# A fused transformer block on one core: first loads on one queue, joint column sums, and four modulation units moved from TensorE to VectorE

## The chip, the cores and the metric

The kernel runs on one core of a Trainium2 chip. The metric is the device time of one execution in microseconds (us). The core has TensorE (PE: matmuls; PEld is its weight load), VectorE (DVE), ScalarE (ACT), GpSimd (POOL), and the queues through which transfers are issued: SP's own (SPq) and ScalarE's (ACTq). Matmuls write to PSUM, eight banks of 128 x 512 float32; everything else lies in SBUF.

## What is computed

The input is x (256 tokens of 1024) and one conditioning row c of 1024. All arithmetic is float32. Cut to what matters here:

```python
mod = silu(c) @ w_ada + b_ada                    # 1024 x 6144, twelve units of 512 columns
shift1, scale1, gate1, shift2, scale2, gate2 = split(mod, 6)
h = rmsnorm(x) * norm1_w * (1 + scale1) + shift1
r_q, r_k, r_v, r_g, d_q, d_k, d_v, d_z, d_a, d_b = split(h @ w_in)
ret = retention(rotary(r_q), rotary(r_k), r_v)   # 4 heads of 128, chunks of 128
qkv = silu(causal_dwconv([d_q, d_k, d_v], conv_w))
dn  = gated_delta_rule(l2norm(q), l2norm(k), v, g, beta)   # inverse of (I + A) per chunk of 64
x = x + gate1 * (concat(ret, dn) @ w_out)
h2 = rmsnorm(x) * norm2_w * (1 + scale2) + shift2
x = x + gate2 * moe(h2)                          # 32 experts, top 2 of one group, 6 MB each
# then a pooling mixer and a convolutional feed-forward layer on the result
```

Units 0 and 1 of `mod` are shift1, 2 and 3 scale1, 4 and 5 gate1, 6 and 7 shift2, 8 and 9 scale2, 10 and 11 gate2.

## The kernel before

The program of each engine is written out by hand, with counting semaphores between the engines (`mm` counts TensorE's finished groups, `vd` VectorE's, `ad` ScalarE's). Tokens lie in two groups of 128 (index n).

**Slots and loads.** Weights come in units of 2 MB into eight slots: five of `ring` (0 to 4; slot 3 is HIGH, slot 4 is FIFTH) and three of `arena`. `units.place` fixes each unit's slot, and `sync_program` (L2392 and on) issues the loads in one written order on SP's queue; before each it waits until the slot's former unit has been used (`used`). The first three transfers (constants C, `first_cols` with c in it, and x) are issued by ScalarE (L1899 to L1901), and SP waits for `first_cols` between units 0 and 1. Behind the modulation units 0 to 3 come the delta units dn 1, dn 0 and dn 2 (keys, queries, values), the small loads, the retention units proj 2, 0, 1, and then modulation units 4 to 7, each once its slot is free.

**A modulation unit on TensorE** (`ada`, L540 to L553). The column of silu(c) is spread to 32 columns (`crep`), and eight matmuls (16 instructions, since one of float32 takes two) leave four partial rows of 512 in four row groups of a PSUM bank. The partial rows are copied to `part` (`spread_out` on VectorE for units 0 to 3, L1252; `ada` on ScalarE for the others, L1909) and summed over partitions by a matmul: with `sel` as weights for the gates (`gate_total`, L556), and for shift and scale with the data as weights, so that the result is a column (`column_total`, L561: eight matmuls of 64 weight columns for each half, over the view `by_eights`, which the copy has put in another order). `turn_over(n)` issues n matmuls whose results nobody reads.

**The start.** TensorE does units 0 to 3 with the transposes of the normed rows between, VectorE makes modc (shift and scale), and both VectorE and ScalarE write hT, the modulated and transposed input.

**Delta projections** (`delta_project`, L604). Twelve blocks of 16 matmuls, dn 1, dn 0, then the small gates `ab`, then dn 2. Behind each block VectorE runs a convolution of four dependent instructions from PSUM (`delta_conv`, L1281 to L1290) and ScalarE a silu. Then come norms, gates and cumulated decays ("gc", "dec", "bt", "at").

**PSUM banks.** `take` hands the banks out in turn; a take waits until the group that had the bank eight takes before (leaving kept ones out) has been read, which its reader tells by `free`. In the order of takes, "dec" of n = 0 and 1 have banks 5 and 6, "bt" 7 and 0, "at" 1 and 2, and the first retention projection 3 and 4. "dec" is read by the eight subtractions at L1331 on VectorE.

**The inverse, in levels.** For each chunk, levels 1 to 6 follow each other: "pm" (TensorE), its copy PM (ScalarE, L2026), "xm" and "xt" (TensorE), and their subtraction from XM and XTD (VectorE, L1393 and L1399). "pm" of a level needs XM of the level before, and the masked factor of its level, which GpSimd makes (`masked`, L2316 on). The retention projections (`project`, 24 matmuls of 512 columns each) are put between as filler for TensorE, and before the change so were units 4 (end of level 2), 5 (level 3), 6 (level 4) and 7 (in level 5 between "pm" and "xm"). The projections use float32 split in two parts: ScalarE makes the high one (`higher`, L1940) and VectorE the low one (`lower`, L1237).

**GpSimd's order** in this stage: `masked(2)`, `masked(3)`, `rotate(0, 0)`, `rotate(0, 1)`, `masked(4)`, `rotate(1, 0)`, `rotate(1, 1)`, `masked(5)`. A `rotate` is six instructions of 128 x 256 on a projected and copied block of queries (0) or keys (1); `turn_rotated` on TensorE waits for both token groups of it. "pm" of level 5 waits for `masked(5)`.

**Behind it** come scores, the output projection, the router, the experts (each of 32 with 6 MB of weights through the eight slots), and the feed-forward layer.

A take, as TensorE does it:

```python
            def take(*name, keep=False):                       # L483
                b, k = banks.take(name, keep)
                if k > 1:
                    pe.wait_ge(bank_free[b], k - 1)
```

## Time and profile before

| what | us |
|---|---|
| three executions | 916.0, 918.78, 918.87 |
| their median | 918.78 |
| the profiled execution | 919.4 |
| its span, first to last instruction | 917.6 |
| TensorE busy in the span | 893.3 (97%) |
| VectorE / ScalarE / GpSimd busy | 410.6 / 314.3 / 106.2 |
| mean share of the 16 DMA engines, by the queues | 80% |

The span is 1.8 us short of the time of the profiled execution. TensorE is busy nearly all the time, so what counts is where it waits, what it does that could be left out, and at which of its two clock levels it does it.

### The profile page before, as it was taken

The page shows a single profiled execution, that of the slowest core. Times are in us where ns is not written, and L with a number is a line of the kernel's source. Part 1 is how long each engine was busy: PE and PEld are TensorE (multiplying, and loading weights), DVE is VectorE, ACT ScalarE, POOL GpSimd, SP SyncE. Part 2 cuts the span into 40 slices and gives each one's busy share as a digit, 9 for nine tenths or more (in the row PEclk, how much of TensorE's full clock was granted, in tenths as well). Part 3 has the DMA queues.
Part 4 walks back from the last instruction along what each step waited for, and adds up shares of the span by engine and source line. Part 5 has one row for each costly group of instructions (what it writes and reads, how often), then busy time and mean ns, then how long its engine had stood idle before and what let it go on. Part 6 is the DMA issues. An engine that isn't in the chain of part 4 may idle for free.

```text
span 917.6 us, 13421 instructions
## 1 busy us (share of the span) xinstructions
PE 893.3 (97%) x5530; PEld 575.9 (63%) x5530; DVE 410.6 (45%) x697; ACT 314.3 (34%) x507; POOL 106.2 (12%) x116
## 2 busy tenths in 40 slices
PE   5999999999999999999999999999998999999998
PEld 2688876777644434444344444444435899999886
DVE  2357725368522323222223232223234778888643
ACT  1227335342522222322222212222213555555531
POOL 1024463031000000000000000000000022222200
PEclk9999999999999999999999999999999999999999
DMA  9962259787999899999999999999999665555301
GB/s 353 415 291 93 93 193 355 282 326 292 398 402 419 313 420 421 421 419 420 420 421 418 419 421 420 423 419 419 421 421 357 217 194 183 180 179 184 128 1 47
DMA packets 60892, 289.47 MB, mean 315 GB/s; under 512 B 4500, under 2 KB 28692, under 8 KB 33688
## 3 DMA queue, kind: packets, MB, share of 16 engines
q1 hardware_dynamic: 59104, 284.13, 78.3%
q10 hardware_dynamic: 1720, 4.40, 1.2%
q8 instruction: 46, 0.75, 0.3%
q14 instruction: 22, 0.18, 0.1%
HBM read 287.47 MB, written 1.05 MB: 314 GB/s over the span
## 4 chain that ended last, share of the span: by engine, by line
PE 90%; DVE 3%; DMA 3%; issue 2%; ACT 1%; POOL 1%; SPq 0%; ACTq 0%; DVEq 0%
PE ps L1032 24%; PE ps L1056 12%; PE ps L537 8%; PE ps L1020 7%; PE ps L1153 7%; PE ps L1154 7%; PE ps L1155 7%; PE ps L620 4%; PE ps L1072 3%; PE ps L1045 2%; DMA ring<-in_ada_units_dram 2%; PE ps L552 2%; PE ps L520 2%; DMA S<-in_first_cols_dram 1%; PE ps L511 1%
## 5 line engine op out<-in xcount | busy, mean ns | idle before, releaser
L1035 PE MATMUL ps<-ring,proj 128*64 128x512 f32 x320 | 140.9, 593 | 0.0
L1032 PE MATMUL ps<-ring,proj 128*64 128x512 f32 x304 | 133.9, 593 | 0.0
L1853 DVE TENSOR_TENSOR w_l<-ring,w_h 128x2048 fp32r<-128x2048 f32 x33 | 75.5, 2292 | 44.8 <-ACT w_h L2201 44.8
L1153 PE MATMUL ps<-h_h,w_h 128*128 128x256 f32 x336 | 95.1, 283 | 0.0
L1154 PE MATMUL ps<-h_l,w_h 128*128 128x256 f32 x336 | 95.1, 283 | 0.0
L1155 PE MATMUL ps<-h_h,w_l 128*128 128x256 f32 x336 | 95.1, 283 | 0.0
L1032 PEld LDWEIGHTS ps<-ring,proj 128*64 128x64 f32 x304 | 41.1, 137 | 84.6 <-issue 84.6
L1032 PE MATMUL ps<-arena,proj 128*64 128x512 f32 x208 | 91.6, 593 | 0.0
L2201 ACT CAST w_h<-ring 128x2048 fp32r<-128x2048 f32 x33 | 62.8, 1903 | 81.4 <-PE ps L1155 76.9
L1709 DVE SCALAR_TENSOR_TENSOR RQ<-ps,gate_of,proj 128x512 f32<-128x512 f32 x32 | 24.0, 751 | 147.1 <-PE ps L1057 147.1
L2157 ACT CAST MX_r<-RQ 64x512 fp32r<-64x512 f32 x62 | 38.2, 616 | 143.9 <-DVE RQ L1709 143.1
L1035 PE MATMUL ps<-arena,proj 128*64 128x512 f32 x192 | 84.6, 593 | 0.0
L1697 DVE COPY proj<-ps 128x256 f32<-128x256 f32 x32 | 13.6, 425 | 132.6 <-PE ps L1045 132.6
L2149 ACT ACTIVATE proj<-ps 64x512 f32<-64x512 f32 x32 | 18.9, 590 | 153.1 <-PE ps L1035 153.1
L1056 PE MATMUL ps<-ring,proj 128*64 128x512 f32 x144 | 65.6, 598 | 0.6 <-issue 0.6
L1020 PE MATMUL ps<-hT,proj 128*128 128x128 f32 x512 | 63.2, 284 | 2.5 <-DVE hT L1674 2.1
L1057 PE MATMUL ps<-ring,proj 128*64 128x512 f32 x144 | 65.6, 598 | 0.0
L1032 PEld LDWEIGHTS ps<-arena,proj 128*64 128x64 f32 x208 | 28.2, 137 | 58.2 <-issue 58.2
L1153 PEld LDWEIGHTS ps<-h_h,w_h 128*128 128x128 f32 x336 | 64.5, 192 | 0.0
L1154 PEld LDWEIGHTS ps<-h_l,w_h 128*128 128x128 f32 x336 | 64.5, 192 | 0.0
L1155 PEld LDWEIGHTS ps<-h_h,w_l 128*128 128x128 f32 x336 | 64.5, 192 | 0.0
L1020 PEld LDWEIGHTS ps<-hT,proj 128*128 128x128 f32 x512 | 61.8, 201 | 2.8 <-DVE hT L1674 2.3
(372 smaller groups left out, 1601.7 us busy)
## 6 DMA issues: line engine op xcount, KB each, us to landing
ring<-in_w_dram SPq DMA_DIRECT2D x114, 1024.0 KB, 15.0
arena<-in_w_dram SPq DMA_DIRECT2D x72, 1024.0 KB, 15.7
ring<-in_ada_units_dram SPq DMA_DIRECT2D x11, 2048.0 KB, 8.6
ring<-in_ffn_w_in_dram SPq DMA_DIRECT2D x22, 1024.0 KB, 8.1
ring<-in_in_units_dram SPq DMA_DIRECT2D x6, 2048.0 KB, 23.1
ring<-in_ffn_w_out_dram SPq DMA_DIRECT2D x5, 2048.0 KB, 8.0
arena<-in_in_units_dram SPq DMA_DIRECT2D x2, 2048.0 KB, 24.8
ring<-in_out_units_dram SPq DMA_DIRECT2D x2, 2048.0 KB, 9.2
```

What stands on the lines that cost most here:

```text
L537: i = pe.matmul(ps[:, 0:512], rows_k, w[:, k, :], start=(first and k == 0), stop=(final and k == 3))
L1020: t = pe.matmul(ps[:, o:o + 128], XR[:, n, c * 128:(c + 1) * 128], pick[:, n, :, :].rearrange("p e s -> p (e s)"), start=(n == 0), stop=(n ...
L1032: pe.matmul(ps[0:SLOTS, :], XTe[i % 2][:, k, :], u1[:, k, :], start=(k == 0), stop=(k == 7))
L1035: t = pe.matmul(ps[64:64 + SLOTS, :], XTe[i % 2][:, k, :], u3[:, k, :], start=(k == 0), stop=(k == 7))
L1056: pe.matmul(ps[0:SLOTS, :], HTe[i % 2][:, k, :], w[:, 0:512], start=(k == 0), stop=(k == 3))
L1057: t = pe.matmul(ps[64:64 + SLOTS, :], HTe[i % 2][:, k, :], w[:, 512:1024], start=(k == 0), stop=(k == 3))
L1153: pe.matmul(ps, ah, bh, start=first, stop=False)
L1154: pe.matmul(ps, ah, bl, start=False, stop=False)
L1155: return pe.matmul(ps, al, bh, start=False, stop=final)
L1853: ve.tensor_tensor(low, src, dst.bitcast(F32), ALU.subtract).then_inc(split_ready, 1)
L2157: ac.copy(YB[i % 2][own, j, :], YG[own, :]).then_inc(E.high_rows, 1)
L2201: ac.copy(dst, src).then_inc(w_high, 1)
```

## The change

- The first loads all go through SP's queue, in the order `first_cols`, C, unit 0, x, unit 1, 2, 3, with no wait between. ScalarE issues none of them.
- The view `by_eights` becomes a strided one, so that units are copied to `part` as they are.
- `column_totals` sums both halves of a segment with eight matmuls of 128 weight columns, in place of sixteen of 64. The start keeps its two halves, and one `turn_over(2)` there goes.
- Units 4 to 7 are computed on VectorE: eight dependent instructions of 128 x 512 each (a product, then seven products with a sum), from the unit's slot into `part`. Then the sum over partitions has `ones` as weights. Units 4 and 5 go between the convolutions, unit 6 into level 1 behind `lower(3)`, unit 7 into level 2 behind `lower(5)`.
- `gate_total` of 4 and 5 moves on TensorE from level 4 to before `project(0)`, on VectorE from level 3 to before level 0.
- Units 4 and 5 are loaded among dn 1, dn 0 and dn 2. The slots are given out anew: behind the retention units the roles of slots 0, 2 and FIFTH are exchanged in a ring, in the experts and the last layer too.

```diff
-        by_eights = part_[...].rearrange("k (c p) -> k c p", c=8)
+        by_eights = part_[...].rearrange("k (p c) -> k c p", c=8)
...
-        for name, s in (..., (("dn", 1), R + 1), (("dn", 0), R),
-                        (("dn", 2), FIFTH), (("proj", 2), 0), (("proj", 0), 1), (("proj", 1), 2), (("ada", 4), FIFTH), (("ada", 5), 0),
-                        (("ada", 6), 1), (("ada", 7), FIFTH), (("proj", 3), 2), (("ada", 10), 0), (("ada", 8), 1), (("ada", 9), FIFTH),
-                        (("proj", 4), 0), (("ada", 11), 2), (("wo", 0), 1), (("wo", 1), FIFTH)):
+        for name, s in (..., (("dn", 1), R + 1), (("ada", 4), 0),
+                        (("dn", 0), R), (("ada", 5), 1), (("dn", 2), FIFTH), (("proj", 2), 2), (("proj", 0), 0), (("proj", 1), 1),
+                        (("ada", 6), FIFTH), (("ada", 7), 2), (("proj", 3), 0), (("ada", 10), FIFTH), (("ada", 8), 1), (("ada", 9), 2),
+                        (("proj", 4), FIFTH), (("ada", 11), 0), (("wo", 0), 1), (("wo", 1), 2)):
...
             def gate_total(j, src):
                 ps = take("total", j)
-                pe.wait_ge(*drained("ada", j))
-                pe.matmul(ps[:, :], sel, src, ...)
+                pe.wait_ge(ada_rows, by_vector.index(j) + 1)
+                pe.matmul(ps[:, :], ones, src, ...)
...
             def column_totals(seg):
-                column_total(seg, 1, column_total(seg, 0))
+                ps = take("columns", seg)
+                ...
+                for c in range(8):
+                    i = pe.matmul(ps[:, 2 * c:2 * c + 2], by_eights[:, c, :], (ones if seg == 3 else sel)[:, 0:2], start=True, stop=True)
...
             second = column_total(1, 0)
-            turn_over(2)
             ada(3, ada_half)
...
                 four(("at", n), ...)
+            gate_total(4, part[0])
+            gate_total(5, part[1])
             project(0)
...
                 elif level == 5:
-                    ada(7)
...
                 elif level == 4:
-                    gate_total(4, part[0])
-                    gate_total(5, part[1])
                     turn_rotated(0)
...
                     project(4)
-                    ada(4)
-                elif level == 3:
-                    ada(5)
                 elif level == 4:
                     turn_rotated(1)
-                    ada(6)
...
+            def ada(j, chunks=range(8)):        # VectorE
+                w, dst = unit(("ada", j), 512), part[j % 2]
+                for c in chunks:
+                    if c == 0:
+                        ...
+                        ve.wait_ge(*filled(("ada", j)))
+                        ve.tensor_scalar(dst, w[:, 0, :], ccol[:, 0:1], None, ALU.mult).then_inc(*vd.up("ada", j))
+                    else:
+                        ve.wait_ge(*vd.of("ada", j))
+                        ve.scalar_tensor_tensor(dst, w[:, c, :], ccol[:, c:c + 1], dst, ALU.mult, ALU.add)...
...
-                ve.tensor_copy(by_eights[:, :, 64 * (j % 2):64 * (j % 2) + 64]..., full("ada", j)...)
+                ve.tensor_copy(part[j % 2], full("ada", j)[:, :]).then_inc(*free("ada", j))
...
-            delta_conv(1, range(4))
-            delta_conv(0, range(4))
+            delta_conv(1, range(1))
+            for m in range(1, 4):
+                delta_conv(1, (m,))
+                ada(4, range(2 * m - 2, 2 * m))
+            for m in range(4):
+                delta_conv(0, (m,))
+                ada(4, (6, 7)) if m == 0 else ada(5, range(2 * m - 2, 2 * m))
             ve.tensor_copy(ab_turned, ...)
             delta_conv(2, (0,))
+            ada(5, (6, 7))
...
+            gate_total(4)
+            gate_total(5)
             idb = mid(cst("ident_half"), 4)
...
                 if level == 1:
                     lower(3)
+                    ada(6)
                 elif level == 2:
                     lower(5)
-                elif level == 3:
-                    gate_total(4)
-                    gate_total(5)
+                    ada(7)
...
-            ac.dma_start(C[:, :], I["consts"][:, 0:258]).then_inc(const_in, 16)
-            ac.dma_start(first_cols, I["first_cols"]).then_inc(first_in, 16)
-            ac.dma_start(X[:, :, :], ...).then_inc(x_in, 16)
...
+            sp.dma_start(first_cols, I["first_cols"]).then_inc(first_in, 16)
+            sp.dma_start(C[:, :], I["consts"][:, 0:258]).then_inc(const_in, 16)
             load_ada(0)
-            sp.wait_ge(first_in, 16)
+            sp.dma_start(X[:, :, :], ...).then_inc(x_in, 16)
             load_ada(1)
...
             load_in("dn", 1, 2560)
+            load_ada(4)
             load_in("dn", 0, 2048)
+            load_ada(5)
             load_in("dn", 2, 3072)
...
             load_in("proj", 1, 512)
-            load_ada(4)
-            load_ada(5)
             load_ada(6)
```

ScalarE's copies of units 4 to 7 go too, and its copies of 8 and 9 become plain ones.

## Rows read from the trace of the kernel before

**Rows 1.** Windows: busy us of each engine with instructions, granted PE clock, DMA share, GB/s

```profile
34.70:82.00 47.30, 47.21 (x222) 38.61 (x222) 25.27 (x60) 20.49 (x35) 8.19 (x17) 1.00 0.57 235
...
500.00:600.00 100.00, 100.00 (x514) 43.98 (x512) 29.24 (x53) 23.02 (x47) 0.00 (x0) 1.00 1.01 421
```

**Rows 2.** Line L2454, second half of unit 3, issued at 11.3 us: time to landing

```profile
DMA to landing us min/median/max: 18.4/18.4/18.4
```

**Rows 3.** Tile arena, 0 to 40 us: loads dn 1 (first) and dn 0, landing

```profile
L2433 SPq DMA_DIRECT2D arena<-in_in_units_dram x2: 452/454/456, 12.0 to 12.5; - x2
DMA to landing us min/median/max: 22.6/24.8/27.0
```

**Rows 4.** Windows of the start, columns as in rows 1

```profile
11.00:12.00 1.00, 1.00 (x6) 0.20 (x8) 0.00 (x0) 0.00 (x0) 0.00 (x0) 1.00 0.75 160
...
14.00:16.00 2.00, 1.90 (x13) 0.69 (x5) 1.04 (x3) 0.28 (x2) 0.91 (x3) 1.00 0.97 410
```

**Rows 5.** VectorE in order of time: start us, us, line, operation

```profile
63.27 0.48 DVE L1285 TENSOR_SCALAR arena<-ps,S 128x256 f32<-128x256 f32 x1 [1.42 <-PE ps L620]
...
71.72 0.17 DVE L1296 COPY S<-ps 128x16 f32<-128x16 f32 x1 [1.76 <-PE ps L638]
```

**Rows 6.** VectorE by form: count, total us, mean ns

```profile
L1317 DVE SCALAR_TENSOR_TENSOR arena<-arena,MX 128x1024 f32<-128x1024 f32 x2 | 2.4, 1220 | 3.4 <-ACT MX L1975 3.4
```

**Rows 7.** TensorE in order of time: start us, us, line, operation

```profile
87.69 3.36 PE L537 MATMUL ps<-ring_r,vrow_r 128*128 128x512 f32 x12
...
99.28 1.15 PE L520 MATMUL ps<-consts,arena 64*64 64x64 f32 x32
...
103.02 1.15 PE L520 MATMUL ps<-arena 64*64 64x64 f32 x32 [0.23 <-POOL arena L2325]
...
127.53 1.92 PE L552 MATMUL ps<-ring,S 128*32 128x512 f32 x16
129.38 1.15 PE L520 MATMUL ps<-arena 64*64 64x64 f32 x32
...
141.16 1.98 PE L559 MATMUL ps<-part,consts 128*128 128x512 f32 x4
...
148.83 1.15 PE L520 MATMUL ps<-arena 64*64 64x64 f32 x32
...
158.44 1.14 PE L752 MATMUL ps<-arena 64*64 64x64 f32 x16
```

**Rows 8.** TensorE, column sums at 172 us (64 weight columns), list sums at 247 us (128)

```profile
172.07 1.82 PE L566 MATMUL ps<-consts,part 128*64 128x2 f32 x32
...
247.27 0.98 PE L926 MATMUL ps<-part,S 128*128 128x32 f32 x8
```

**Rows 9.** VectorE in order of time, 89 and 122 us

```profile
89.69 2.15 DVE L1331 TENSOR_SCALAR arena<-ps,S 128x128 f32<-128x128 f32 x8
...
122.59 2.69 DVE L1240 TENSOR_TENSOR ring_r<-ring,ring_r 128x2048 fp32r<-128x2048 f32 x1
```

**Rows 10.** GpSimd in order of time, levels 2 to 4

```profile
118.76 2.84 POOL L2337 TENSOR_TENSOR S<-proj,S 128x256 f32<-128x256 f32 x4 [10.54 <-ACT proj L1987]
...
123.21 4.75 POOL L2337 TENSOR_TENSOR S<-proj,S 128x256 f32<-128x256 f32 x4
...
129.41 1.41 POOL L2325 TENSOR_TENSOR arena<-arena,consts 128x256 f32<-128x256 f32 x2
135.21 2.80 POOL L2337 TENSOR_TENSOR S<-proj,S 128x256 f32<-128x256 f32 x4 [4.38 <-ACT proj L1987]
...
143.83 1.42 POOL L2325 TENSOR_TENSOR arena<-arena,consts 128x256 f32<-128x256 f32 x2
```

**Rows 11.** ScalarE in order of time, the copy of "pm" of level 5

```profile
150.05 0.65 ACT L2026 COPY arena<-ps 128x256 f32<-128x256 f32 x2
```

**Rows 12.** Windows around a wait of TensorE in the experts, columns as in rows 1

```profile
488.90:491.00 2.10, 0.07 (x1) 0.00 (x0) 0.48 (x3) 0.18 (x1) 0.00 (x0) 1.00 0.99 414
491.00:497.00 6.00, 5.93 (x35) 5.85 (x36) 1.39 (x4) 1.93 (x6) 0.00 (x0) 0.72 1.01 415
```

More of the change, by code:

```diff
@@ L557, in gate_total @@
                 ps = take("total", j)
-                pe.wait_ge(*drained("ada", j))
-                pe.matmul(ps[:, :], sel, src, start=True, stop=True).then_inc(*mm.up("total", j))
+                pe.wait_ge(ada_rows, by_vector.index(j) + 1)
+                pe.matmul(ps[:, :], ones, src, start=True, stop=True).then_inc(*mm.up("total", j))
             def column_total(seg, half, ps=None):
@@ L571, in column_totals @@
             def column_totals(seg):
-                column_total(seg, 1, column_total(seg, 0))
+                ps = take("columns", seg)
+                for half in range(2):
+                    if seg == 3:
+                        pe.wait_ge(ada_rows, by_vector.index(2 * seg + half) + 1)
+                    else:
+                        pe.wait_ge(*drained("ada", 2 * seg + half))
+                for c in range(8):
+                    i = pe.matmul(ps[:, 2 * c:2 * c + 2], by_eights[:, c, :], (ones if seg == 3 else sel)[:, 0:2], start=True, stop=True)
+                i.then_inc(*mm.up("columns", seg, 0))
+                mm.at["columns", seg, 1] = mm.n
             def eights(src, c):
@@ L794, in tensor_program @@
                     ada(10)
-                else:
+                elif level == 6:
                     project(7)
@@ L1910, in ada @@
                 ps, dst = full("ada", j), part[j % 2]
[L1911 to L1915 removed]
+                if j in (8, 9):
+                    ac.wait_ge(*mm.of("columns", 3, 1))
                 elif j > 9:
                     dst = late_part[j % 2]
[L1918 to L1924 removed]
+                ac.copy(dst, ps[:, :]).then_inc(*free("ada", j))
             ac.wait_ge(*vd.of("scale1"))
```

40 lines of the change are left out of this document (15 added, 25 removed).

## The prediction

> **What bounds the kernel now.** I read the windows first. From 34.7 us on TensorE is busy for 47.21 of 47.30 us, and in the experts for 100 of 100 us, while the DMA share is 0.57 and 1.01 [rows 1]. So work taken from TensorE ahead of the experts shortens the run, unless something else is then late. In the experts both TensorE and the transfers are full. Their loads start when slots come free in TensorE's order, and the slots there are only renamed, so I take the experts and all behind them to shift rigidly with the start of the experts.
>
> Next the start. The second half of unit 3 is issued at 11.3 us and lands 18.4 us later, at 29.7 [rows 2]. The first delta unit, dn 1, is issued at 12.0 and lands at 34.6 [rows 3], just when the first delta projection starts (34.67). The sum of unit 3 and the delta load end together, and each must be earlier for a gain.
>
> Then TensorE in order of time [rows 7] and, beside it, GpSimd [rows 10] and VectorE [rows 5, 9]. TensorE runs from 103 to 158 us with no wait. GpSimd works from 118.76 to 130.82 on the first two rotations and `masked(4)`, is idle to 135.21, and works to 145.25 on the last two rotations and `masked(5)` [rows 10]. "pm" of level 5, which needs `masked(5)`, starts at 148.83 [rows 7]. This slack of 3.6 us is what the change uses up.
>
> Measurements of this kernel tell about 0.3%, 2.8 us, from no change. All times below are on the clock of the profiled execution before.
>
> **The start.** With one queue and no wait, the dip at 11 to 12 us goes: 160 GB/s where 410 are moved soon after [rows 4], 0.25 MB or 0.6 us. The order of the other bytes is nearly as before. Bounds: nothing, if x now stands ahead of what it used to run beside; and 2.8 us, as follows. From 12.0 to 34.6 us some 9.3 MB move at 410 GB/s, but units 1 to 3 and dn 1 are only 8.4 MB; 0.9 MB, 2.2 us, is of later loads that run ahead on some of the engines [rows 3, 4]. If the single queue ended that too, it would be 0.6 + 2.2. I take 0.7 us, near the lower end, because those loads are all on SP's queue before as well. The plain copies and the `turn_over(2)` less lie where TensorE waits for unit 3: nothing.
>
> By the Trainium skill (DMA: Bandwidth & Descriptors, "Issuing engines are not separate DMA queues") transfers of all issuing engines run on the same 16 DMA engines and interleave; by that, putting them on one queue would give no more than the dip.
>
> **VectorE among the convolutions.** A chunk of a unit is a product with a sum over 128x512, both inputs in SBUF. The same operation over 128x1024 takes 1.22 us [rows 6]; halved, with some 0.16 us of fixed time, it is 0.69, and 0.72 from one to the dependent next. Before a convolution VectorE is idle for 1.42 us, waiting for TensorE's block [rows 5]; two chunks take 1.44. The sixteen chunks thus just fit. The last two fall between the convolution that ends at 70 us and the copy at 71.72 us [rows 5], which feeds the gates and then, by ScalarE, VectorE and GpSimd, all up to level 1. The loads fit as well: unit 4 comes 5 us (2 MB) behind dn 1, and dn 0, before at 39.5 [rows 3], at 44, ahead of its first block, the fifth. The small loads land 10 us later, and GpSimd's angles with them, which nothing needs before the rotations. I take nothing here; the bounds are 0 and +4 us (a rival below).
>
> **Joint sums.** Thirty-two loads of 64 weight columns take 1.82 us; eight of 128 columns take 0.98 [rows 8], 0.11 us each, so the new sixteen take 1.8 to 1.9. No gain from the joint sums of segments 3 and 4.
>
> **Gate totals.** They cost TensorE 1.8 us at level 4 (the sum at 141.16, 1.98 with its tail) [rows 7] and the same before `project(0)`. But two takes more there turn the banks: `project(0)` gets banks 5 and 6, those of "dec" 0 and 1, where it had 3 and 4. "dec" 1 is freed when the eight subtractions end at 89.69 + 2.15 = 91.84 us [rows 9]. The totals end at 87.69 + 1.82 = 89.51, so TensorE waits for 2.3 us. Both projections then take 99.28 - 87.69 = 11.59 us less some 0.3 of waiting for low parts: "xm" of level 0 comes at 103.1, 3.8 later than before. As 0.23 us of wait at 103.02 go, level 1 is 3.6 us late [rows 7]. Slots and the low part fit; VectorE's additions of the totals (1.3 us) lie in its idle time before "xm".
>
> **Units 4 to 7 off TensorE.** Each is 129.38 - 127.53 = 1.85 us [rows 7], 7.4 in all, of which three (4, 5, 6) and the totals' 1.8 lie before "pm" of level 5. By TensorE alone that "pm" would be at 148.83 + 3.6 - 5.6 - 1.8 = 145.0.
>
> **GpSimd's chain decides instead.** It starts with the rotation at 118.76 + 3.6 = 122.4. While VectorE makes the low part at 122.59, 2.69 us with two inputs in SBUF, four of GpSimd's operations take 4.75 us instead of 2.84 [rows 9, 10]: GpSimd stands still until VectorE's instruction ends. Unit 7 follows right behind this low part: eight such instructions, 5.3 us. GpSimd then has some eight operations of 0.7 us left up to the end of `masked(4)`. I take them to alternate, one of each, so that unit 7 costs GpSimd all of its 5.3 us. `masked(4)` ends at 122.4 + 12.06 + 5.3 = 139.8; the last two rotations and `masked(5)`, 145.25 - 135.21 = 10.04 us, end at 149.8. "pm" of level 5 starts at 149.85, 1.0 later than before, after nearly 5 us of almost no work on TensorE (about 145.1 to 149.8; a last transpose of 0.5 lies in it). No row shows short instructions of both against each other: the bounds are 0 and 5.3 us of delay for GpSimd, of which 2.5 would be hidden.
>
> The Trainium skill (SBUF — State Buffer, "SBUF: two separate sides") has it that a VectorE instruction with two SBUF inputs and a GpSimd one exclude each other for a whole instruction, whichever starts first. The row of the long instruction agrees; by the rule the short ones alternate too, and that speaks against unit 7 there.
>
> **Level 5.** Unit 7 also filled TensorE's wait for ScalarE's copy of "pm". It goes (-1.85), and 0.8 us of wait for the copy (0.65 us and 0.14 ahead of it) shows [rows 11]. "pm" of level 6 is at 149.85 + 9.61 - 1.05 = 158.4, against 158.44 [rows 7]. The 7.4 us are all given back: 3.6 at the banks and 4.8 at GpSimd, against 7.4 + 1.8 less 0.8.
>
> **The clock.** After 2.1 us almost without work in the experts, the granted clock of the next 6 us is 0.72, in part the lower level of 1.2 GHz [rows 12]: 0.28 x 6 = 1.7 us lost. The new idle stretch is twice as long, so I add 1.7 us (bounds 0 and 3.4, if the 2.3 us at `project(0)` cost as much once more).
>
> **Sum.** Start -0.7, to level 6 0.0, clock +1.7: +1.0. Against the profiled execution (919.4, span 917.6 and 1.8 around it) 920.4; the median of the runs is 0.6 lower, so I predict **919.7**. Its own range, with -1.7 or +1.7 for the clock and up to -0.7 more at the start, is 917.3 to 921.5.
>
> **Rivals.**
> 1. *GpSimd is not held by the short instructions*, or gets several of its own between two of VectorE's. For: VectorE's chunks depend on each other and leave small gaps. Against: the 1.9 us lost beside one long instruction. Then `masked(4)` is in time, the rotations start 1.85 - 3.6 later than before, at 137.0, and "pm" of level 5 is at 147.05: 2.8 us less, 916.9, and 915.2 if the clock also holds. Chance 0.18.
> 2. *The clock does not fall*: 918.0. For: a transpose lies in the gap. Chance 0.12.
> 3. *The start gives 2.8 us*: 917.6. Both the sum of unit 3 and dn 1 must profit. Chance 0.08.
> 4. *VectorE is late at the copy of 71.72 us* (slower). If a chunk takes e us more than 0.72, or waits for GpSimd's twelve angle operations of about 0.5 us which by their loads now fall among the convolutions, the lag adds up block by block: 16 e less 0.5. At e = 0.25 it is 3.5 us, and the chain through gates and decays to level 1 is late by as much: 923.2. It decides from e = 0.15 on. Against: the operation is of a known kind. Chance 0.13.
> 5. *All is covered*: the takes find free banks and GpSimd is in time; 7.4 + 0.7 less 0.8 come through, 911.5. Against: the order of banks is fixed by the program. Chance 0.04.
>
> The forecast keeps 0.45.
>
> **How the numbers follow.** 8 in 10 cases lie between 915.2 (rival 1 with the clock held) and 923.0 (rival 4). Faster by over 0.3% means below 916.0: half of rival 1, rival 5, and rivals 1 to 3 together, 0.21. Slower means above 921.5: rival 4 and the upper end of the forecast, two falls of the clock, 0.17. The rest, 0.62, is within 0.3%.
>
> **What the changed profile would show.** Right: the second half of unit 3 landing near 29.0 and dn 1 near 33.9; a wait of 2 us or more of TensorE before `project(0)`, released by VectorE's L1331 group; GpSimd's two rotations of queries 5 us longer; TensorE idle before the second `turn_rotated` and "pm" of level 5, released by GpSimd; a granted clock below 1 behind it; chunks of 0.7 us. Wrong: no wait at the banks, GpSimd as fast as before beside unit 7, the copy of gates later than TensorE's sums, or transfers that land nearly 3 us earlier. If the experts end by another amount than they start, rigid shift is wrong.

## The result and the profile after

The changed kernel takes 930.32 us (median of 4 executions, 929.45 to 931.98) against 918.83 for the kernel before beside it (4 executions): ratio 1.0129, 95% interval 1.0104 to 1.0155. I had predicted 919.7 within 915.2 to 923.0. The prediction was wrong: the kernel is some 12 us slower. Single executions of over 1100 us, one each in e1, e10 and e16 below, are left out everywhere.

| what | before | after |
|---|---|---|
| profiled execution / its span, us | 919.4 / 917.6 | 930.94 / 929.1 |
| TensorE busy, us | 893.3 | 903.6 |
| VectorE / ScalarE / GpSimd busy, us | 410.6 / 314.3 / 106.2 | 433.5 / 310.1 / 110.1 |

TensorE loses four modulation units of 1.85 us and is yet busy for 10 us more. TensorE of the changed kernel, in order of time (start us, us, line, operation, idle before it and its releaser), answers to [rows 7, 8]:

```profile
34.39 2.08 PE L567 MATMUL ps<-consts,part 128*64 128x2 f32 x16
36.40 1.56 PE L507 MATMUL ps<-consts 128*128 128x256 f32 x6
...
91.15 1.88 PE L560 MATMUL ps<-part,consts 128*128 128x512 f32 x4
95.28 3.00 PE L538 MATMUL ps<-ring_r,vrow_r 128*128 128x512 f32 x12 [2.25 <-issue]
...
109.96 1.15 PE L521 MATMUL ps<-arena 64*64 64x64 f32 x32
...
149.69 0.66 PE L528 MATMUL ps<-consts,proj 128*128 128x128 f32 x4 [1.17 <-POOL proj L2348]
151.21 1.82 PE L521 MATMUL ps<-arena 64*64 64x64 f32 x32 [0.87 <-POOL arena L2333]
153.92 3.64 PE L521 MATMUL ps<-arena 64*64 64x64 f32 x48 [0.89 <-ACT arena L2038]
...
162.53 1.14 PE L763 MATMUL ps<-arena 64*64 64x64 f32 x16
...
176.06 3.74 PE L580 MATMUL ps<-consts,part 128*128 128x2 f32 x16
179.72 3.64 PE L553 MATMUL ps<-ring,S 128*32 128x512 f32 x16
183.29 2.08 PE L512 MATMUL ps<-arena 128*128 128x128 f32 x8
185.16 1.26 PE L718 MATMUL ps<-proj 128*128 128x128 f32 x8
```

The joint sum of segment 3 (L580) takes 3.74 us where the two halves took 1.82 [rows 8]. Unit 8 behind it (L553) takes 3.64 where a unit took 1.92 [rows 7]. The wait at the banks is there (2.25 before 95.28), and so are the waits for GpSimd before level 5. The row names no releaser for the first ("issue"), but VectorE's subtractions of "dec" 1 end at 93.03 + 2.15 = 95.18, just before it ends (VectorE in order of time):

```profile
93.03 2.15 DVE L1355 TENSOR_SCALAR arena<-ps,S 128x128 f32<-128x128 f32 x8
```

Windows of the changed kernel behind that sum (columns as in rows 1) show the granted clock fall from full to the lower of TensorE's two levels, while the engine is busy all the time:

```profile
176.00:178.00 2.00, 2.00 (x11) 2.00 (x10) 0.00 (x0) 0.60 (x1) 0.00 (x0) 1.00 0.69 131
178.00:180.00 2.00, 2.00 (x12) 1.91 (x16) 0.17 (x1) 0.00 (x0) 0.00 (x0) 0.69 0.74 311
180.00:182.00 2.00, 2.00 (x12) 0.40 (x8) 0.00 (x0) 0.00 (x0) 0.00 (x0) 0.50 1.04 434
182.00:184.00 2.00, 2.00 (x11) 0.71 (x4) 0.00 (x0) 0.57 (x1) 0.00 (x0) 0.50 0.41 172
```

TensorE's weight loads by form (line, operation, count, total us, mean ns), of the kernel before and then of the changed one, say where the sum's time goes:

```profile
L566 PEld LDWEIGHTS ps<-consts,part 128*64 128x64 f32 x128 | 7.5, 138 | 2.5 <-issue 1.4 <-DVE part L1256 1.1
```

```profile
L567 PEld LDWEIGHTS ps<-consts,part 128*64 128x64 f32 x64 | 8.0, 216 | 1.1 <-issue 0.7 <-DVE part L1275 0.3
L580 PEld LDWEIGHTS ps<-consts,part 128*128 128x128 f32 x32 | 7.8, 333 | 0.1
```

The total is the time in which at least one load ran. It is less than count times mean (128 x 0.138 = 17.7 us against 7.5), since the loads overlap in the record, so total over count is what a load adds. It has doubled for 64 columns (7.5 us / 128 = 0.059 before, 8.0 / 64 = 0.125 after). For 128 columns the kernel before has no such sum, but e6 below has one with its columns side by side: 3.9 / 32 = 0.12 us there against 7.8 / 32 = 0.24 here.

```profile
L576 PEld LDWEIGHTS ps<-consts,part 128*128 128x128 f32 x32 | 3.9, 191 | 0.2
```

The one thing that changed in it is the view `by_eights`: weight column p of sum c was value 128 c + p of the row, and is now value 8 p + c, so a load picks values eight apart.

Five moments of TensorE's order cut the run into stages that can be compared from run to run: where the code of a stage is the same it repeats within 0.5 us, except where the clock falls in it (P; up to 1 us from L6 to V; 1.5 us from P to L1 in e1; V to end). P is the first delta projection, L1 and L6 are "pm" of levels 1 and 6, V is the first transpose behind segment 3's sum and unit 8 (L709 before, L718 after). Each number is a start from the order of time of one profiled execution, or a difference of two:

| kernel | P | P to L1 | L1 to L6 | L6 to V | V to end |
|---|---|---|---|---|---|
| before | 34.67 | 68.35 | 55.42 | 18.23 | 740.93 |
| after | 37.95 | 72.01 | 52.57 | 22.63 | 743.94 |
| difference | +3.28 | +3.66 | -2.85 | +4.40 | +3.01 |

The sum is +11.5 us. My steps said -0.7, +3.6, -1.9 (-3.6, and the clock's 1.7), 0 and 0, together the +1.0 of the prediction.

### The profile page after: what moved, and what is told of

Read it like the earlier page. It is cut to its first block, busy times and chain, and to the rows that moved or that the text cites. A ratio compares the mean times of both kernels' runs of the same rounds, so it can differ in the third digit from the quotient of the medians.

```text
span 929.1 us, 13245 instructions
## 1 busy us (share of the span) xinstructions
PE 903.6 (97%) x5430; PEld 588.3 (63%) x5430; DVE 433.5 (47%) x729; ACT 310.1 (33%) x503; POOL 110.1 (12%) x116
## 4 chain that ended last, share of the span: by engine, by line
PE 90%; POOL 3%; DVE 3%; DMA 2%; issue 2%; ACT 1%; SPq 0%; DVEq 0%; POOLq 0%; ACTq 0%
PE ps L1035 23%; PE ps L1059 12%; PE ps L538 7%; PE ps L1023 7%; PE ps L1158 6%; PE ps L1157 6%; PE ps L1156 6%; PE ps L629 4%; PE ps L1075 3%; PE ps L1048 2%; PE ps L553 2%; DMA ring<-in_ada_units_dram 2%; POOL S L2345 2%; PE ps L521 1%; PE ps L512 1%
## 5 line engine op out<-in xcount | busy, mean ns | idle before, releaser
L1035 PEld LDWEIGHTS ps<-ring,proj 128*64 128x64 f32 x304 | 41.1, 137 | 84.6 <-issue 84.6
```

The source lines that it names most:

```text
L1035: pe.matmul(ps[0:SLOTS, :], XTe[i % 2][:, k, :], u1[:, k, :], start=(k == 0), stop=(k == 7))
```

## The experiments

Fifteen runs followed, each beside the kernel before. "Cost" is (ratio - 1) x 918 us, with the interval of the ratio likewise. The stages are from the one profiled execution of each.

| run | from | cost, us (95%) | P | P to L1 | L1 to L6 | L6 to V | V to end |
|---|---|---|---|---|---|---|---|
| changed kernel, first measurement | | +11.8 (9.5 to 14.2) | 37.95 | 72.01 | 52.57 | 22.63 | 743.94 |
| a0_after, the same again | after | +13.1 (10.5 to 15.7) | 36.71 | 71.98 | 52.59 | 21.59 | 745.13 |
| e1_contig | after | +5.1 (3.0 to 7.2) | 33.67 | 73.47 | 58.72 | 18.13 | 739.01 |
| e2_loads_back | after | +10.8 (8.0 to 13.7) | 35.50 | 71.99 | 52.57 | 21.48 | 745.56 |
| e3_totals_later | after | +9.2 (6.3 to 12.0) | 34.79 | 69.91 | 54.07 | 21.68 | 741.65 |
| e4_unit7_pe | after | +8.1 (5.5 to 10.6) | 34.95 | 72.00 | 50.19 | 22.53 | 740.93 |
| e5_b_strided | before | +11.9 (9.6 to 14.1) | 40.70 | 68.06 | 55.41 | 21.61 | 742.12 |
| e6_b_joint | before | +0.8 (-0.6 to 2.3) | 35.84 | 68.44 | 55.42 | 18.15 | 738.95 |
| e7_b_loads | before | -0.3 (-1.8 to 1.3) | 34.96 | 68.45 | 55.41 | 18.24 | 737.34 |
| e10_b_twice | before | +11.5 (8.5 to 14.5) | 41.30 | 67.93 | 55.41 | 21.79 | 744.97 |
| e13_b_stride2 | before | +0.4 (-0.9 to 1.7) | 34.35 | 68.16 | 55.43 | 18.28 | 738.78 |
| e14_b_stride4 | before | +12.6 (10.4 to 14.8) | 38.79 | 68.45 | 55.41 | 21.58 | 742.17 |
| e9_c_t_7 | after | -4.5 (-6.2 to -2.8) | 35.06 | 69.89 | 50.30 | 18.26 | 736.99 |
| e12_swap | e9_c_t_7 | -6.1 (-8.2 to -3.9) | 34.50 | 69.88 | 48.74 | 18.23 | 737.75 |
| e15_swap_67 | e12_swap | -4.5 (-6.2 to -2.8) | 33.83 | 69.79 | 51.17 | 18.16 | 736.85 |
| e16_swap_loads | e12_swap | -5.9 (-7.7 to -4.0) | 34.35 | 69.88 | 48.74 | 18.23 | 737.90 |

V to end has to be read with care. Behind V the four kernels with the code of before (before, e6, e7, e13) differ only in the form of one sum, and they take 737.34 to 740.93 us. What differs is the granted clock far behind that sum: it falls twice in before (0.96 over the 40 us from 237 on, 0.98 over the 100 us from 477 on), once in e6 and e13 (the second), and not in e7. Among profiles with the same number of these falls, a strided or doubled sum of segment 4 costs 2.6 to 4.6 us.

My theory from these rows: weight columns eight values apart load at half speed, and the clock falls behind the sums. The rivals: the new order of the first loads, or the joint form of the sums, costs the time.

### e1_contig: weight columns side by side again

```diff
-        by_eights = ... .rearrange("k (p c) -> k c p", c=8)
+        by_eights = ... .rearrange("k (c p) -> k c p", c=8)
 # VectorE, units 6 and 7 (the copies of the other units reorder, as before)
+                if j > 5:
+                    w = w.rearrange("k c (p e) -> k c p e", e=8)
+                    dst = by_eights[:, :, 64 * (j % 2):64 * (j % 2) + 64].rearrange("k c p -> k p c")
```

> The changed kernel with the weight columns of the column sums side by side again (the reordering copies are back, VectorE writes units 6 and 7 in that order; the joint 128-column sums stay). Theory A, weight columns eight values apart load at half speed: the eight matmuls of a half (64 weight columns) take about 1.1 us instead of 2.08, those of a joint sum (128) about 1.9 instead of 3.74, the clock stays near full behind them, the delta projections start near 34.7 us instead of 37.95, pm of segment 3 is built 3.5 to 4.5 us earlier and segment 4's 3 us more: 919 to 922 us. Theory B, the new order of the first loads starves or cools TensorE at the start: the projections still start near 38 and only what the later sums lose comes back: 924 to 927 us. Theory C, a joint sum of 128 columns is what is slow, strided or not: it stays near 3.7 us and the time at 927 us or more.

Measured: cost +5.1 us, so 7 of the change's 12 go with the view. TensorE in order of time, at segment 3's sum and at level 5:

```profile
143.57 1.15 PE L521 MATMUL ps<-arena 64*64 64x64 f32 x32 [3.00 <-POOL arena L2342]
...
151.99 0.90 PE L528 MATMUL ps<-consts,proj 128*128 128x128 f32 x4 [3.65 <-POOL proj L2357]
...
179.37 1.84 PE L580 MATMUL ps<-consts,part 128*128 128x2 f32 x16
181.14 1.92 PE L553 MATMUL ps<-ring,S 128*32 128x512 f32 x16
```

The joint sum takes 1.84 us and the clock holds behind it: the stage L6 to V is 18.13, that of before. P is at 33.67, 4.3 earlier than in the changed kernel. Theories B and C fall. Against the changed kernel e1 gives back 13.7 us in P, L6 to V and V to end, and loses 7.6 in the two stages between. From P to L1 it is 1.5 us: the bank wait is as long as in the changed kernel, but this time the clock falls behind it (0.50 from 92 to 94 us, where in the changed kernel it stayed at 1.00), and the projection takes 4.54 us where it took 3.00:

```profile
90.92 4.54 PE L538 MATMUL ps<-ring_r,vrow_r 128*128 128x512 f32 x12 [2.27 <-issue]
```

The stage L1 to L6 grew to 58.72 us, which no theory expected. VectorE now writes units 6 and 7 scattered, and GpSimd is slowed beside it. VectorE and then GpSimd in order of time:

```profile
115.20 8.29 DVE L1265 SCALAR_TENSOR_TENSOR part<-ring,S,part 128x512 f32<-128x512 f32 x7
...
130.89 10.52 DVE L1265 SCALAR_TENSOR_TENSOR part<-ring,S,part 128x512 f32<-128x512 f32 x7
```

```profile
122.89 7.46 POOL L2354 TENSOR_TENSOR S<-proj,S 128x256 f32<-128x256 f32 x4 [10.89 <-ACT proj L2008]
```

A chunk of unit 6 takes 8.29 / 7 = 1.18 us, nearly all of them while GpSimd is idle; in e3, with plain writes, seven take 5.48, 0.78 each. So VectorE ends unit 6 later, and its low part and then unit 7 fall on GpSimd's rotations: four operations take 7.46 instead of 2.84 [rows 10].

### e2_loads_back: the first loads on two queues

```diff
+            ac.dma_start(C[:, :], I["consts"][:, 0:258]).then_inc(const_in, 16)
+            ac.dma_start(first_cols, I["first_cols"]).then_inc(first_in, 16)
+            ac.dma_start(X[:, :, :], I["x"]...).then_inc(x_in, 16)
 # SP: the same three removed, sp.wait_ge(first_in, 16) behind load_ada(0)
```

> The changed kernel with the first loads on two queues again, SP's sequencer waiting for the first columns as before. Theory A (strided weight loads set the start, unit 3 lands in time either way): delta projections still near 37.5 to 39 us, the time within 1 us of the changed kernel's 930.3. Theory B (the order of the first loads is what costs the start its 3.3 us): the projections come back to 34.7 us and the time to 927.

Measured: cost +10.8, within the interval of the changed kernel; P at 35.50, neither 34.7 nor 37.5 to 39, so both theories miss it. The time sides with theory A: the order of the loads does not explain the 12 us. What P differs by is at least in part the clock, for the same start of the code has P at 37.95, 36.71, 34.79 and 34.95 in the four profiles of after, a0_after, e3 and e4.

### e3_totals_later: gate totals behind the projections

```diff
-            gate_total(4, part[0])
-            gate_total(5, part[1])
             project(0)
             project(1)
+            gate_total(4, part[0])
+            gate_total(5, part[1])
```

> The changed kernel with the two gate totals behind projections 0 and 1 instead of before them. My theory of the bank: TensorE no longer stands idle 2.25 us at 93.0 for VectorE's read of the total's bank, project(0) starts about 2.5 us earlier, and the time falls by 2 to 2.5 us to about 928. The rival: VectorE's or GpSimd's masked copies, which read the projections, or the levels' chain behind them take the gain, and the time stays within 0.5 us.

TensorE in order of time:

```profile
87.91 3.39 PE L538 MATMUL ps<-ring_r,vrow_r 128*128 128x512 f32 x12
...
99.46 1.88 PE L560 MATMUL ps<-part,consts 128*128 128x512 f32 x4
```

No wait stands before the projections, and P to L1 shrinks by 72.01 - 69.91 = 2.10 us: the wait goes with the order of the takes, as I had worked it out. But L1 to L6 grows by 1.50. The waits before level 5 are the same there (1.12 and 0.87 us for GpSimd, 0.99 for ScalarE); the granted clock is not: 0.74 from 140 to 160 us against 0.83 in the changed kernel, 1.8 us in 20. By the stages the edit brings 0.6 us. The cost is 2.6 us less than the changed kernel's, but the two intervals overlap, and in this profile P alone is 3.2 earlier at a granted clock of 1.00 up to there. So a gain in the whole time is not shown.

### e4_unit7_pe: unit 7 on TensorE and ScalarE

```diff
-        by_vector = (4, 5, 6, 7)
+        by_vector = (4, 5, 6)
 # TensorE, behind "pm" of level 5; ScalarE likewise
+                elif level == 5:
+                    ada(7)
 # segment 3's sums in halves: sel for unit 7, ones for unit 6
```

> The changed kernel with modulation unit 7 on TensorE and ScalarE again, in level 5, and segment 3's sums in two halves. If GpSimd's rotations are held by unit 7's instructions on VectorE (rotate 5.82 us instead of 4.75, masked copies 2.34 instead of 1.41), GpSimd's last masked copy ends 4 to 5 us earlier, TensorE's waits between 143.7 and 154 (0.36, 1.17, 0.87 us) go, and 1.85 to 2.1 us of TensorE work for the unit come in their place: the time within 1 us of 930.3. The rival, that GpSimd's hold moves more than those waits: the time falls by 2 us or more.

Measured: L1 to L6 is 50.19 against 52.57, 2.4 us less although TensorE does 1.85 more: by this stage the rival holds (the intervals of the whole time overlap, and P differs by the clock). The granted clock of 140 to 160 us is 1.00 (0.83 in the changed kernel, 3.4 us lost), so most of what the edit gives comes as clock. GpSimd in the changed kernel beside unit 7, then in this run without it, and last VectorE's unit 7 in the changed kernel:

```profile
130.17 5.82 POOL L2345 TENSOR_TENSOR S<-proj,S 128x256 f32<-128x256 f32 x4
136.07 1.08 POOL L2347 TENSOR_TENSOR proj<-S 128x256 f32<-128x256 f32 x1
137.11 1.19 POOL L2348 TENSOR_TENSOR proj<-S 128x256 f32<-128x256 f32 x1
138.26 2.34 POOL L2333 TENSOR_TENSOR arena<-arena,consts 128x256 f32<-128x256 f32 x2
```

```profile
127.17 4.75 POOL L2356 TENSOR_TENSOR S<-proj,S 128x256 f32<-128x256 f32 x4
131.99 0.73 POOL L2358 TENSOR_TENSOR proj<-S 128x256 f32<-128x256 f32 x1
132.68 0.74 POOL L2359 TENSOR_TENSOR proj<-S 128x256 f32<-128x256 f32 x1
133.38 1.43 POOL L2344 TENSOR_TENSOR arena<-arena,consts 128x256 f32<-128x256 f32 x2
```

```profile
133.16 7.98 DVE L1262 SCALAR_TENSOR_TENSOR part<-ring,S,part 128x512 f32<-128x512 f32 x7
```

The two engines do hold each other: VectorE's seven chunks of unit 7 in the changed kernel (the last row) take 7.98 us (1.14 each) beside them, against 5.48 (0.78) for unit 6 without. One chunk and one operation of GpSimd pass in some 1.15 us, where the two alone add up to 0.78 + 0.73 = 1.5. From the first rotation to the end of `masked(4)` GpSimd needs 14.9 us with unit 7 and 12.1 without it: unit 7 costs it 2.8 us, not the 5.3 I had taken. The expectation that its last masked copy would end 4 to 5 us earlier was wrong: counted from L1 it ends at 40.4 us against 41.1, since the last two rotations now wait 2.5 us for ScalarE. Of TensorE's waits before level 5 there remain 0.57 and 0.86 of 1.17 and 0.87; the 0.89 for ScalarE goes, filled by unit 7.

### e5_b_strided and e6_b_joint: the two halves of the sums' change, each alone on the kernel before

e5 has the new `by_eights` with the plain copies of VectorE and ScalarE, halves apart. e6 has the old view and copies, and for segments 3 and 4:

```diff
-                column_total(seg, 1, column_total(seg, 0))
+                ps = take("columns", seg)
+                for half in range(2):
+                    pe.wait_ge(*drained("ada", 2 * seg + half))
+                for c in range(8):
+                    i = pe.matmul(ps[:, 2 * c:2 * c + 2], by_eights[:, c, :], sel[:, 0:2], start=True, stop=True)
+                i.then_inc(*mm.up("columns", seg, 0))
```

> The kernel before, with nothing but the order of the modulation rows changed: plain copies of VectorE and ScalarE, and weight columns eight values apart in the column sums; halves stay apart. Theory A (weights eight apart load at half speed and the clock falls behind them): the sums of 32 matmuls take 3.6 to 3.7 us instead of 1.82 at segments 3 and 4, the start loses 1 to 3 us, matmuls behind the sums run at half clock for 3 to 5 us; 923 to 927 us in all. The rival, that the sums cost what they did and the loss lies in the joint form or in what goes to VectorE: within 1 us of before.

> The kernel before with joint column sums of segments 3 and 4, 128 weight columns side by side. By the run with reordered rows such a sum takes 1.84 us against 1.82 in halves, so the time is within 0.5 us of before. The rival: the first half's sum hid work or a wait, or the longer weight loads lower the clock: 1 us or more slower.

e6 costs nothing that can be measured. e5 takes 928.93 us, cost +11.9, a little over what I expected and as much as the whole change. (That the two are equal is chance in part: the rest of the change adds and takes away about as much.) TensorE in order of time, e5:

```profile
177.81 3.55 PE L566 MATMUL ps<-consts,part 128*64 128x2 f32 x32
181.28 3.43 PE L552 MATMUL ps<-ring,S 128*32 128x512 f32 x16
```

The sum doubles, and unit 8 behind it runs at the lower clock, with no other part of the change present. At the start, four such sums and the clock behind them move P from 34.67 to 40.70.

### a0_after: the changed kernel once more

> The changed kernel itself once more, as the yardstick on this chip. If its 930.3 us are the kernel's, it takes 929 to 932 us; if part of them was a clock that fell at the start of its first execution (projections at 37.95 us, where two kernels with the same start had them at 34.8 and 34.95), it takes 926 to 928 us, with the projections near 34.8.

929.53 us, cost +13.1: the loss is the kernel's, and so is the slow start (P at 36.71), though the size of the slow start varies.

### e10_b_twice: the sums' matmuls twice, side by side

Each column sum of the kernel before is computed twice over into the same place.

```diff
-                for c in range(8):
+                for c in list(range(8)) * 2:
                     i = pe.matmul(ps[64 * half:64 * half + 64, 2 * c:2 * c + 2],
```

> The kernel before, its weight columns side by side as they were, but each column sum computed twice, so that the weight loads of a sum take as long as the strided ones did (16 matmuls of 64 weight columns in about 2.1 us) while the stride is not there. If the clock falls behind any long run of matmuls that move two columns each, this costs what the strided view alone cost, 10 to 12 us. If the clock falls because of something in the strided loads themselves, only the added matmuls are paid: 4 us at the start less what waits there, and 2 times 1.8 us later, 5 to 7 us in all.

Cost +11.5 us, what the stride cost. TensorE in order of time, and the windows behind (columns as in rows 1):

```profile
178.27 3.69 PE L566 MATMUL ps<-consts,part 128*64 128x2 f32 x64
181.89 3.62 PE L552 MATMUL ps<-ring,S 128*32 128x512 f32 x16
```

```profile
180.00:182.00 2.00, 2.00 (x42) 1.98 (x44) 0.01 (x1) 0.00 (x0) 0.00 (x0) 0.98 0.72 270
182.00:184.00 2.00, 2.00 (x12) 0.51 (x15) 0.16 (x1) 0.00 (x0) 0.00 (x0) 0.50 0.99 426
```

So the length of the sums is enough for the whole cost; nothing else about the stride is needed. Each sum adds 1.0 us (the four of the start) or 1.87 us (the two later ones), 7.7 in all and part of it in what were waits; the rest is the clock. It falls at the end of a sum of 3.7 us in which TensorE mostly loads weights and moves two columns per load (in the changed kernel already in its last 2 us, 0.69), and in the same place with one kind of long sum and with the other. Behind the same sum of 1.8 us in the kernel before it did not fall.

### e7_b_loads: the first loads on one queue, alone

```diff
+            sp.dma_start(first_cols, I["first_cols"]).then_inc(first_in, 16)
+            sp.dma_start(C[:, :], I["consts"][:, 0:258]).then_inc(const_in, 16)
             load_ada(0)
-            sp.wait_ge(first_in, 16)
+            sp.dma_start(X[:, :, :], I["x"]...).then_inc(x_in, 16)
```

> The kernel before with nothing but the order of the first loads changed: all on one queue, as in the changed kernel. My prediction's step says 0.7 us earlier at the first delta projection (34.67 before) and 0.5 to 1 us off the time, where the clock holds. The rival: TensorE turns the constants over early, then stands idle until unit 0 lands near 10 us, and runs the first modulation unit at half clock (3.64 us instead of 3.20), which takes the gain or more: 0 to 1.5 us slower.

Cost -0.3 (-1.8 to 1.3), P at 34.96. The constants now come first, and TensorE waits for unit 0 behind them:

```profile
3.66 2.08 PE L506 MATMUL ps<-consts 128*128 128x256 f32 x4 [3.66 <-DMA consts<-in_consts_dram]
10.32 3.61 PE L552 MATMUL ps<-ring,S 128*32 128x512 f32 x16 [4.58 <-DMA ring<-in_ada_units_dram]
```

The granted clock of 10 to 20 us is 0.86 (1.00 before). Neither a gain nor a loss is shown; the earlier landing and the lower clock may cancel.

### e13_b_stride2, e14_b_stride4: how far apart the columns may lie

```diff
-        by_eights = ... .rearrange("k (c p) -> k c p", c=8)
+        by_eights = ... .rearrange("k (a p t) -> k a p t", a=8 // T, t=T)   # T = 2, 4
-                                  by_eights[:, c, 64 * half:64 * half + 64], ...
+                                  by_eights[:, c // T, 64 * half:64 * half + 64, c % T], ...
```

The reordering copies of VectorE and ScalarE write in this order.

> The kernel before, whose reordering copies now leave the weight columns of a sum two values (8 bytes) apart instead of side by side. If any stride halves the load speed: the sums of segments 3 and 4 take 3.5 to 3.6 us instead of 1.82 and the time is 10 to 12 us longer, as with stride eight. If the loss grows with the distance, a stride of two costs less: sums of 1.8 to 2.5 us and the time within 3 us of before.

> The kernel before, whose reordering copies leave the weight columns of a sum four values (16 bytes) apart. A stride of two cost 0.05 us in a sum of 1.82 (the sums of 32 matmuls took 1.87) and no time in all; a stride of eight doubled the sum and cost 12 us. If the load speed falls from a stride of four on: sums of 3.5 us and 927 to 929 us. If it falls only beyond 16 bytes: sums under 2.0 us and the time within 1 us of before.

Weight loads by form, a stride of two (e13), of four (e14) and of eight (e5):

```profile
L566 PEld LDWEIGHTS ps<-consts,part 128*64 128x64 f32 x128 | 7.7, 138 | 1.8 <-issue 1.1 <-DVE part L1256 0.7
```

```profile
L566 PEld LDWEIGHTS ps<-consts,part 128*64 128x64 f32 x128 | 14.9, 215 | 1.8 <-issue 1.1 <-DVE part L1256 0.7
```

```profile
L566 PEld LDWEIGHTS ps<-consts,part 128*64 128x64 f32 x128 | 14.9, 216 | 1.8 <-issue 1.1 <-DVE part L1256 0.7
```

The cost is a step, not a slope: 7.7 us for 128 loads at 8 bytes apart (7.5 side by side), 14.9 at 16 bytes and at 32. By the Trainium skill (SBUF — State Buffer, in "Door 1: The DMA port swizzle") SBUF has lines of 16 bytes and full bandwidth needs at least two accesses to a line. The runs agree for weight loads: with two fp32 values to a line the load is fast, with one it is half as fast. The same place says that one may stride over 4 fp32 for free; that does not agree, and the measurement decides.

The factor of two is shown for these matmuls of float32 only. The kernel before has loads eight values apart elsewhere, in the transposes over the view `eights`. Weight loads by form and TensorE in order of time, transposes from columns eight apart (X, MX) and side by side (proj):

```profile
L527 PEld LDWEIGHTS ps<-consts,X 128*128 128x128 f32 x16 | 2.0, 193 | 0.7 <-DVE X L1473 0.6
L527 PEld LDWEIGHTS ps<-consts,proj 128*128 128x128 f32 x16 | 1.8, 141 | 0.6 <-issue 0.5
```

```profile
20.29 2.06 PE L527 MATMUL ps<-consts,MX 128*128 128x128 f32 x16
142.98 1.04 PE L527 MATMUL ps<-consts,proj 128*128 128x128 f32 x8
```

The load itself takes 193 ns instead of 141, but a transpose takes 0.13 us either way. The longer load was thus to be seen in the kernel before, though not its cost.

### e9_c_t_7, e12_swap, e15_swap_67, e16_swap_loads: what is left of the change without its faults

e9 is e1, e3 and e4 together.

> The changed kernel with three edits together: weight columns side by side, gate totals behind projections 0 and 1, unit 7 on TensorE. Summed from the runs that did one each: projections at 33.7 us (1.0 earlier than before), level 1 at 103.6 us, masked level 6 near 154 to 155 us (before 158.44), sums of segments 3 and 4 as before with the full clock behind them: 913 to 915 us, faster than both kernels. The rival: unit 6, written by VectorE in the reordered rows (1.2 us an instruction instead of 0.77), holds GpSimd's rotations in its turn, and the clock falls in the waits: 917 us or more.

Ratio 0.9951 (0.9932 to 0.9969): 912.40 us, 4.5 faster than before and a little better than the 913 to 915 added up from the parts. L1 to L6 takes 50.30 us. At level 5 GpSimd still ends last (TensorE in order of time):

```profile
144.13 0.66 PE L528 MATMUL ps<-consts,proj 128*128 128x128 f32 x4 [0.74 <-POOL proj L2368]
145.65 1.15 PE L521 MATMUL ps<-arena 64*64 64x64 f32 x32 [0.86 <-POOL arena L2353]
```

e12 orders GpSimd by that, and TensorE and ScalarE with it:

```diff
 # GpSimd, level 3 (masked(5) was at level 4)
                     rotate(1, 0)
+                    masked(5)
                     rotate(1, 1)
 # TensorE behind "pm" of level 5, and ScalarE
                     ada(7)
+                    turn_rotated(1)
```

> The version of 912.4 us (weight columns side by side, totals behind the projections, unit 7 on TensorE) with GpSimd's masked copies of level 5 moved ahead of its last rotation, and the turn of that rotation's rows moved behind unit 7 on TensorE and ScalarE. TensorE's waits of 0.74 and 0.86 us on GpSimd before level 5 go: 1 to 1.6 us faster, 911 us. The rival: the last rotation is then late for the turn of its rows or the scores, and nothing is gained.

```profile
142.49 1.15 PE L521 MATMUL ps<-arena 64*64 64x64 f32 x32 [0.26 <-issue]
143.56 1.92 PE L553 MATMUL ps<-ring,S 128*32 128x512 f32 x16
```

Both waits are gone, L1 to L6 takes 1.56 us less, and the kernel takes 910.86 us, ratio 0.9934 (0.9911 to 0.9958): faster than both kernels.

e15 gives unit 6 back to TensorE (`by_vector = (4, 5)`, `ada(6)` at level 4).

> The version of 910.9 us with modulation unit 6 on TensorE and ScalarE as well, so that VectorE keeps units 4 and 5 alone. TensorE gets 1.9 us more; against that, VectorE's eight instructions of unit 6 no longer hold GpSimd's first rotation (7.47 us instead of 2.86). If TensorE is what bounds the levels, 1.5 to 2 us slower, 912.5 us; if the hold was on the path after all, the same or faster.

L1 to L6 takes 51.17, 2.4 us more, though GpSimd's first four operations are back at 2.84 us (7.47 in e9). Of it 1.85 is the unit and 0.84 a wait for a modulation unit's load behind level 5, less the 0.26 that go before "pm" of level 5. By this stage unit 6 is worth its place on VectorE; the intervals of the whole times overlap. e16 is e12 with the loads of e2.

> The version of 910.9 us with the first loads on two queues again, as in the kernel before. One queue alone gave 0.5 us with a wide interval (granted clock 0.86 at 10 to 20 us, 1.00 before). If TensorE's early idle and its lower clock give back what the earlier landing of unit 3 brings: within 0.5 us of 910.9. If the order of the loads is worth the 0.7 us of my prediction's step: 911.6 us.

Ratio 0.9936 against 0.9934: no difference by the order of the first loads can be measured here either.

## Why the prediction was wrong

Point by point, by its own steps.

**Joint sums, and the plain copies: the step that failed.** I wrote "the new sixteen take 1.8 to 1.9" and put the plain copies at nothing; the sixteen take 3.74, and the four sums of the start 2.08 instead of 1.09. The first number came from eight loads of 128 columns at 247 us [rows 8], whose columns lie side by side; the new ones lie eight apart. I counted columns and not how they lie. The diff's first line changed exactly that, and I read it as a matter of the copies. Joint or not makes no difference (e6); the view alone costs 11.9 us (e5). In the changed kernel the matmuls themselves are 1.9 us longer in each of segments 3 and 4, and 1 us in each of the four sums of the start, part of it in what had been waits.

**The clock behind the sums.** I looked for a fall of the clock only behind waits, and none of my rivals had one behind a busy stretch. Unit 8 and the transposes behind it lose 1.7 and 0.9 us after segment 3's sum; with the sum's 1.9 that is the +4.40 to within 0.2. In V to end the +3.01 hold 1.9 of segment 4's sum, and the clock behind it (0.50 from 214 to 216 us). e10 shows that a sum made long in another way brings it too. The upper bound that I had named, a fall behind the bank wait as well, did not occur in the changed kernel but did in e1.

**The start.** The transfers did what I had said. The second half of unit 3, issued at 4.51 us, lands at 28.8 (29.7 before, 29.0 foreseen), and dn 1, issued at 5.00, at 33.8 (34.6 before, 33.9 foreseen). A gain of 0.7 us is not shown for all that. Where the sums are short P is at 33.67 to 35.06 under the new order (e1, e7, e9, e12, e15) and at 34.35 to 35.84 under the old one (before, e6, e13, e16), and e7 costs -0.3 (-1.8 to 1.3). The spread within each is larger than the step.

With strided sums TensorE became what bounds the start: at 31.48 us the last unit follows without a wait, where before TensorE had waited 1.0 us for unit 3. "Where TensorE waits for unit 3: nothing" held only as long as the work hidden there was the shorter. The size of the loss is the clock's: in e3 and e4, with the strided sums but a granted clock of 1.00, P is at 34.79 and 34.95, within the range of the short sums, and in the changed kernel, with 0.74 from 20 to 30 us, at 37.95. The clock can fall there without long sums too (e6: 0.85 from 20 to 30 us). So of the +3.28 a part is this one profile's bad luck.

**VectorE among the convolutions.** Right. A chunk takes 0.75 to 0.77 us (I took 0.72), and the copy at 71.72 [rows 5] is at 75.10, 3.38 later, which is the 3.28 of the start and 0.1. Rival 4 did not occur.

**The banks.** Right: 2.25 us of wait against my 2.3, and the stage 3.66 longer against 3.6. e3 takes the wait away and finds 2.1.

**GpSimd's chain.** The mechanism was right and the size off: unit 7 costs GpSimd 2.8 us up to `masked(4)`, not 5.3, since a chunk and an operation pass in less than their sum (unit 7 alone would take VectorE 6.0 us, as unit 6 does from 117.30 to 123.30, not 5.3), and 0.4 more in the rotation behind it (3.22 us instead of 2.80). "pm" of level 5 starts 41.25 us behind level 1 (151.21 - 109.96), where I had put 149.85 - 106.6 = 43.2. TensorE's waits there are 1.17 and 0.87 us for GpSimd and 0.89 for ScalarE's copy (I had put 0.8). The fall of the clock was deeper: 0.62 from 150 to 156 us and 0.72 from 156 to 160, 0.38 x 6 + 0.28 x 4 = 3.4 us at most, where I had put 1.7. From "pm" of level 5 to that of level 6 it takes 11.32 us, where I had put 8.56 and the 1.7. So the stage is 2.0 shorter and 1.1 longer than I said, -2.85 against -1.9. The two errors partly cancel.

**The rigid shift.** Right as far as the profiles can tell. Segment 4's sum and the clock behind it account for the +3.01, and the code behind V repeats no better than within 3.6 us by those far falls of the clock.

Of the range: it was built on bounds for every step that I had called unknown, and the step that failed was one that I had called known.

## What to carry to other kernels

When a change alters only a view, look at who reads it: as TensorE weights of fp32 matmuls, values 16 bytes apart cost twice the load time of values 8 bytes apart or side by side. Before a duration is taken from a row of the same operation, its access pattern must be the same and not only its shape. Where a reordering copy is already hidden, it is cheaper than a strided read that is not. And look behind a stretch of weight loads that got longer: here sums of 3.6 to 3.7 us were followed by the lower clock and cost about as much again there, and the same sums of 1.8 us were not.

## What the runs showed of the hardware beyond that

- The weight loads' cost in fp32 matmuls is a step between 8 and 16 bytes: 0.060, 0.116 and 0.116 us a load of 64 columns at strides of two, four and eight (7.7, 14.9 and 14.9 us for 128). Transposes from columns eight apart take no longer than others (0.13 us each).
- TensorE's clock fell while it was never idle. In the changed kernel it was 1.00 in the first 2 us of a sum of 3.7, 0.69 in the next 2 and 0.50 from 180 to 184 us; in e10 it was 0.98 in the last 2 us of the sum and 0.50 from 182 to 184.
- VectorE's product with a sum over 128x512 takes 0.78 us with all operands in order, and 1.18 where the running sum is read and written in permuted order (e1).
- Short instructions of VectorE and GpSimd slow each other: 0.78 to 1.14 us a chunk, 0.74 to 1.08 and 1.19 for GpSimd's.
